# The modulation of an AdaLN layer moved from GpSimd to TensorE's column tiles

## The reference

```python
def adaln(cvec, w, b):
    m = jax.nn.silu(cvec) @ w + b          # w: 1024 x 3072
    return jnp.split(m, 3, axis=-1)

# layer i of the second block
sh_l, sc_l, gt_l = adaln(c, ada_w[i], ada_b[i])
h_lat = rms_norm(x_lat, norm_g[i]) * (1.0 + sc_l[:, None]) + sh_l[:, None]
# layer 0 also, for the context tokens:
sh_c, sc_c, gt_c = adaln(c_ctx, ada_w[i], ada_b[i])
```

## Time and profile before

| | |
|---|---|
| median of 3 runs | 2357.45 us (2355.15 to 2359.11) |
| the profiled execution | 2356.58 us, its span 2354.9 us |
| mean granted TensorE clock | 0.963 |
| PE busy | 2177.0 us, 92% of the span |
| DVE busy | 1459.5 us, 62% |
| ACT busy | 782.6 us, 33% |
| POOL busy | 285.3 us, 12%, 196 instructions |
| moved by DMA | 164.5 MB |

### The profile page before, as it was taken

The page is one execution under the profiler, slowest core; times in us unless marked ns, Lnnn a source line. Parts: engine busy times, 40 slices in busy tenths (PEclk is TensorE's granted clock), DMA queues, the critical chain, the costliest instruction groups (busy, mean ns, idle before and its releaser), DMA issues.

```text
span 2354.9 us, 26875 instructions
## 1 busy us (share of the span) xinstructions
PE 2177.0 (92%) x10667; PEld 1741.9 (74%) x10667; DVE 1459.5 (62%) x2256; ACT 782.6 (33%) x1161; POOL 285.3 (12%) x196
## 2 busy tenths in 40 slices
PE   6998878888999999799999999999999798999998
PEld 4876666566888886687888888887877577687876
DVE  5623778637848583477777777777777632443342
ACT  4362222334324333423333332233222233332232
POOL 0012666414224030000000000000000000000000
PEclk9998899998999999899999999999999799999998
DMA  4331111323434343111111111111111022023320
GB/s 139 99 89 37 45 38 53 90 88 109 126 110 132 115 129 87 45 54 45 46 46 48 51 45 47 52 45 46 45 47 53 18 89 81 28 85 85 87 82 37
DMA packets 311132, 164.54 MB, mean 70 GB/s; under 512 B 6268, under 2 KB 307938, under 8 KB 311010
## 3 DMA queue, kind: packets, MB, share of 16 engines
q1 hardware_dynamic: 311010, 162.85, 23.8%
HBM read 160.73 MB, written 2.10 MB: 69 GB/s over the span
## 4 chain that ended last, share of the span: by engine, by line
PE 72%; DVE 19%; issue 5%; ACT 3%; POOL 0%; SPq 0%; DMA 0%; DVEq 0%; ACTq 0%; POOLq 0%
PE bank L474 16%; PE bank L476 16%; PE bank L475 16%; DVE KC L1710 3%; DVE MT L1732 3%; DVE QC L1712 3%; DVE QQ L1717 2%; PE bank L819 2%; PE bank L509 2%; PE bank L493 1%; PE bank L491 1%; PE bank L492 1%; PE bank L885 1%; PE bank L798 1%; DVE PP L1725 1%
## 5 line engine op out<-in xcount | busy, mean ns | idle before, releaser
L1344 DVE TENSOR_TENSOR wl<-stage,wh 128x1024 fp32r<-128x1024 f32 (+1 forms) x248 | 311.7, 1258 | 661.9 <-ACT wh L947 661.8
L474 PE MATMUL bank<-hh,wh 128*128 128x512 f32 x1408 | 586.3, 416 | 30.6 <-DVE hl L1365 14.7
L947 ACT ACTIVATE wh<-stage 128x1024 fp32r<-128x1024 f32 (+1 forms) x248 | 260.1, 1050 | 964.3 <-PE bank L476 610.0
L476 PE MATMUL bank<-hh,wl 128*128 128x512 f32 x1408 | 554.4, 394 | 0.0
L475 PE MATMUL bank<-hl,wh 128*128 128x512 f32 x1408 | 553.1, 393 | 0.0
L474 PEld LDWEIGHTS bank<-hh,wh 128*128 128x128 f32 x1408 | 267.2, 190 | 97.2 <-issue 36.8
L476 PEld LDWEIGHTS bank<-hh,wl 128*128 128x128 f32 x1408 | 266.9, 190 | 58.9
L475 PEld LDWEIGHTS bank<-hl,wh 128*128 128x128 f32 x1408 | 268.3, 191 | 52.9 <-issue 4.3
L474 PE MATMUL bank<-gh,wh 128*128 128x512 f32 x432 | 179.4, 415 | 16.0 <-DVE gl L1573 6.6
L428 POOL TENSOR_TENSOR mprod<-stage,gs 128x1024 f32<-128x1024 f32 x64 | 130.8, 2044 | 465.6 <-DMA stage<-in_ada_w 460.7
L476 PE MATMUL bank<-gh,wl 128*128 128x512 f32 x432 | 170.6, 395 | 0.0
(11 more groups left out here) (305 smaller groups left out, 3188.3 us busy)
## 6 DMA issues: line engine op xcount, KB each, us to landing
stage<-in_hg_w_in SPq DMA_DIRECT2D x80, 512.0 KB, 3.6
stage<-in_ada_w SPq DMA_DIRECT2D x48, 512.0 KB, 3.6
stage<-in_w_up SPq DMA_DIRECT2D x44, 512.0 KB, 3.8
stage<-in_ft_w_in SPq DMA_DIRECT2D x32, 512.0 KB, 3.9
stage<-in_w_in SPq DMA_DIRECT2D x28, 512.0 KB, 3.8
stage<-in_w_down SPq DMA_DIRECT2D x16, 512.0 KB, 3.7
stage<-in_hg_w_out SPq DMA_DIRECT2D x16, 512.0 KB, 3.6
stage<-in_ft_w_out SPq DMA_DIRECT2D x16, 512.0 KB, 3.5
```

The lines of the kernel that those rows point to most:

```text
L474: pe.matmul(bank[t % NLIN][:], wh[:, s, k, :], xh[:, k, :], start=a, stop=False)
L476: mm = pe.matmul(bank[t % NLIN][:], wl[:, s, k, :], xh[:, k, :], start=False, stop=b)
L947: do(A.activation(wh[:, l % NSPLIT, 0:nk, :], stage[:, u["slot"], 0:nk, :], ACT.Copy), "hi_ready")
L1344: do(X.tensor_tensor(wl[:, l % NSPLIT, 0:nk, :], stage[:, u["slot"], 0:nk, :], wh[:, l % NSPLIT, 0:nk, :].bitcast(F32), ALU.subtract), f"s ...
```

## The change

GpSimd's program goes. A raw unit becomes a tile of 512 rows and 256 columns of `ada_w` (same bytes, pieces of 1 KB instead of 512 bytes); two of them, the upper and lower half of the rows, make a block, and there are 12 blocks a layer. `silp` holds the silu of both vectors as columns 0 and 1 of 32, the other 30 zero, for each of the eight row tiles. PE takes `silp` as the stationary operand with 32 columns and the raw weights as the moving operand with 256 columns, both plain f32; the four row tiles of a half go to four column tiles of the array (32 output partitions each), the second half accumulates on the first. ScalarE copies the 128 x 256 sums out of `bank[7]` (`mod_rows`), and two matmuls with the constant `pick` (`mod_columns`) add the four partial sums and turn rows into columns. PE frees the slot now. In the mixer a block stands in 12 of 32 steps and its column matmuls one step later; in the FFN a block stands between the two tiles of each of the first twelve pairs, and its column matmuls behind the next pair's first tile. ScalarE's copy stands behind the evacuation of the pair's second tile.

```diff
+BLOCKS = 12
-    raws = [dict(w="ada_w", layer=l, rows=(0, 8), col=j * P, lin=False, raw=l * 24 + j)
-            for l in range(2) for j in range(24)]
+    raws = [dict(w="ada_w", layer=l, rows=(4 * kh, 4), col=j * 2 * P, lin=False, raw=(l * BLOCKS + j) * 2 + kh)
+            for l in range(2) for j in range(BLOCKS) for kh in range(2)]
...
             for half in range(2):
                 add("w_up", (0, 8), half * FF + j * P, "h")
-            units.extend(late[:2 if j < 2 else 1])
-            late = late[2 if j < 2 else 1:]
+                if half == 0:
+                    units.extend(late[:2])
+                    late = late[2:]
...
+        MOD_STEP = {2 + (8 * j) // 3: j for j in range(BLOCKS)}
...
-        @block.gpsimd
-        def _(pool):
-            do = Own(pool, "pool_chain")
...
# PE, a raw unit
+                    j, kh = u["raw"] // 2, u["raw"] % 2
...
+                    pe.wait_ge(S(f"stage_in{slot}"), 16 * (u["load"] + 1))
+                    if kh == 0 and j:
+                        pe.wait_ge(S("mod_ev"), j)
+                    w = raw_view(u)
+                    for k in range(4):
+                        mm = pe.matmul(bank[7][32 * k:32 * k + 32, 0:2 * P], silp[:, 4 * kh + k, :], w[:, k, :],
+                                       start=(kh == 0), stop=(kh == 1))
+                    mm.then_inc(S(f"stage_free{slot}"), 1)
...
+            def mod_columns(j):
+                pe.wait_ge(S("mod_ev"), j + 1)
+                for i in range(2):
+                    c = 2 * P + 2 * (2 * j + i)
+                    mm = pe.matmul(bank[7][:, c:c + 2], modrow[:, j % 2, i * P:(i + 1) * P], pick, start=True, stop=True)
+                mm.then_inc(S("mod_mm"), 1)
...
             def modulation(step):
-                while not units[pos[0]]["lin"] and modulation_sums(units[pos[0]]["raw"] + 1) <= 1.3 * (step + 1):
-                    unit(units[pos[0]])
-                    pos[0] += 1
+                if step - 1 in MOD_STEP:
+                    mod_columns(MOD_STEP[step - 1])
+                if step in MOD_STEP:
+                    for _ in range(2):
+                        unit(units[pos[0]])
+                        pos[0] += 1
...
# PE, the FFN
-                    units_to(t0 + 2 * j + 1, ("h_ready", KT) if r == 0 and j == 0 else None)
+                    units_to(t0 + 2 * j, ("h_ready", KT) if r == 0 and j == 0 else None)
+                    if 1 <= pairs + j <= BLOCKS:
+                        mod_columns(BLOCKS + pairs + j - 1)
+                    units_to(t0 + 2 * j + 1)
...
# ScalarE
+            def mod_rows(j):
+                u = raw_last[j]
+                act.wait_ge(S(f"stage_free{u['slot']}"), u["load"] + 1)
+                if j >= 2:
+                    act.wait_ge(S("mod_mm"), j - 1)
+                do(A.activation(modrow[:, j % 2, :], bank[7][:, 0:2 * P], ACT.Copy), "mod_ev")
...
+                    if p < BLOCKS:
+                        mod_rows(BLOCKS + p)
```

More of the change, by code:

```diff
@@ L96, in host_constants @@
                                 np.sin(2 * np.pi * (np.outer(t, u[1:-1]) % T) / T)], 1)).astype(np.float32)
-    onecol = np.zeros((P, 31), np.float32)
-    onecol[:, 15] = 1.0
-    return {"cf": cf, "hm": hm, "dch": dch, "dtok": dtok, "onecol": onecol}
+    pick = np.zeros((P, 2), np.float32)
+    pick[np.arange(4) * 32, 0] = pick[np.arange(4) * 32 + 1, 1] = 1.0
+    return {"cf": cf, "hm": hm, "dch": dch, "dtok": dtok, "pick": pick}
 def make_units():
@@ L203, in build @@
         raw = at("raw", A0 + 56, [P, 2, T + 8])
-        mprod = at("mprod", A0 + 56, [P, KT, P])
-        mod = at("mod", A0 + 60.25, [P, 2, 2, P])
+        modrow = at("modrow", A0 + 60.25, [P, 2, 2 * P])
+        silp = at("silp", A0 + 73, [P, KT, 32])
         cst = at("cst", A0 + 62.25, [P, 2 * P])
@@ L273, in build @@
         bank = [ctx.enter_context(nc.psum_tensor(f"bank{i}", [P, 512], F32)) for i in range(8)]
+        mcol = bank[7][:, 2 * P:2 * P + 96]
         def vcol(name, i=0):
@@ L279, in build @@
         halfeps = small[:, 0:1]
-        onecol = small[:, 1:32]
+        pick = small[:, 1:3]
         ada = small[:, 32:128]
@@ L288, in build, with raw_view @@
         mx, nmx, den, rden = gs[:, 160:192], gs[:, 192:224], gs[:, 224:256], gs[:, 256:288]
-        silc = gs[:, 288:304]
         block = ctx.enter_context(nc.Block())
+        def raw_view(u):
+            return view(stage[:, u["slot"], 0, 0:1], [[2 * P, 4], [1, 2 * P]])
         def tile_last(t):
@@ L301, in build @@
         T_OUT, T_UP, T_HG, T_HO, T_FT = FIRST["w_out"], FIRST["w_up"], FIRST["hg_w_in"], FIRST["hg_w_out"], FIRST["ft_w_in"]
+        MOD_STEP = {2 + (8 * j) // 3: j for j in range(BLOCKS)}
+        raw_last = {u["raw"] // 2: u for u in units if not u["lin"]}
         ffn_tiles = []
@@ L355, in load @@
             def load(u):
-                w = d["ada_w_2"][u["layer"]] if u["w"] == "ada_w" else weights[u["w"]]
                 k0, nk = u["rows"]
+                if u["w"] == "ada_w":
+                    sp.dma_start(raw_view(u), d["ada_w_2"][u["layer"]][k0 * P:(k0 + nk) * P, u["col"]:u["col"] + 2 * P].rearrange(
+                        "(k p) c -> p k c", p=P)).then_inc(S(f"stage_in{u['slot']}"), 16)
+                    return
+                w = weights[u["w"]]
                 sp.dma_start(stage[:, u["slot"], 0:nk, :],
@@ L449, in unit @@
                 if not u["lin"]:
+                    j, kh = u["raw"] // 2, u["raw"] % 2
+                    if u["raw"] == 0:
+                        pe.wait_ge(S("silc_ready"), 2)
                     if u["raw"] == 24:
                         pe.wait_ge(S("ada0"), 1)
[L453 to L459, removed]
+                    pe.wait_ge(S(f"stage_in{slot}"), 16 * (u["load"] + 1))
[6 more added lines that the diff above has]
+                    mm.then_inc(S(f"stage_free{slot}"), 1)
                     return
@@ L710, in _ @@
             attention_tail(32)
+            modulation(32)
             weigh(7)
@@ L1105, in heads4, with modulated @@
                 return b[:].rearrange("p (h c) -> p h c", c=P)
+            def modulated(n):
+                if n in MOD_STEP:
+                    mod_rows(MOD_STEP[n])
             for c in range(TT):
@@ L1116, in _ @@
                 do(A.activation(G["xx"][:], heads4(bank[4]), ACT.Copy), "x1e")
+                modulated(8 * c)
                 for l in range(1, 7):
@@ L1121, in _ @@
                     weights(8 * c + l)
+                    modulated(8 * c + l)
                 act.wait_ge(S("uw"), c + 1)
@@ L1128, in _ @@
                 do(A.activation(oT[:, :, tok], heads4(bank[4]), ACT.Copy), "o_ev")
+                modulated(8 * c + 7)
             attention_tail(32)
@@ L1386, in _ @@
             do(X.memset(halfeps, EPS), "const_set")
+            do(X.memset(silp[:], 0.0), "silp_zero")
             for k in range(KT):
@@ L1576, in _ @@
             bias = ROWS["ada_b"][0]
-            dve.wait_ge(S("mod_mm"), modulation_sums(24))
-            do(X.tensor_tensor(ada[:, 0:48:2], bank[7][:, 0:48:2], V[:, bias:bias + 24], ALU.add))
-            do(X.tensor_tensor(ada[:, 1:32:2], bank[7][:, 1:32:2], V[:, bias:bias + 16], ALU.add), "ada0")
+            dve.wait_ge(S("mod_mm"), BLOCKS)
+            do(X.tensor_tensor(ada[:, 0:48:2], mcol[:, 0:48:2], V[:, bias:bias + 24], ALU.add))
+            do(X.tensor_tensor(ada[:, 1:32:2], mcol[:, 1:32:2], V[:, bias:bias + 16], ALU.add), "ada0")
             do.settle()
```

11 lines of the change are left out of this document (6 added, 5 removed).

## The result

The changed kernel takes 2336.09 us (median; 2334.99 to 2337.88), the kernel before on the same chip 2358.28 (2355.15 to 2361.14). The ratio is 0.9907, with a 95% interval of 0.989 to 0.9924: 0.9% faster, where 1.4% slower was forecast. 2336 is outside the range and about 1 us from what rival C gave.

A forecast was written before the change was run, and what follows sets the result against it. TensorE was taken to bound the FFN, and hand-offs between engines the mixer. FFN +35.7, mixer -4.5 and the round's end +1 summed to +32.2 us, giving 2390 us, 1.4% slower than 2357.45; range 2342 to 2404.

The forecast's parts named there:

- rival C: Raw blocks on TensorE: all four column tiles run together, 0.86 us a block, total 2335 us; chance 0.17.
- New PE work: Raw blocks in mixer and FFN: 3.43 us each, column tiles one after another; column matmuls 0.46 us (FFN) or 0.60 (mixer).
- GpSimd's work goes: Mixer: VectorE loses some 39 us of stretching, TensorE's idle time falls by 18 us; FFN gains nothing except at round ends.
- Old PE work goes: Old modulation-sum matmuls leave TensorE: 23.9 us less in the mixer, 11.0 us less in the FFN.
- The FFN's sum: FFN: 12 x (3.43 + 0.46) - 11.0 = +35.7 us, undamped because TensorE is full there.
- The mixer's sum: Mixer: 227.5 us TensorE work plus 29 idle, less 11 for a better clock, gives 245.5 against 250, -4.5 us.
- The loads and ScalarE: Weight loads and ScalarE's copies: loads covered by 5 us, column matmuls hardly covered, counted zero; first FFN round's end +1 us.

The follow-up runs named there:

- e1: Changed kernel with all eight row tiles of a block summed in column tile 0 instead of spread over four: 2392.72 us, 1.0143 of the kernel before.
- e2: Kernel before with GpSimd's three instructions a sum cut to one column of each tile, waits kept, modulation sums not computed: 2331.26 us, ratio 0.9886.
- e7: Changed kernel plus 40 rounds of GpSimd's old three operations on an unread buffer, in the mixer alone: 2352.67 us, 0.9973 of the kernel before.
- e5: Changed kernel with all 24 blocks of both layers in the mixer and none in the FFN: 2330.83 us, 0.9885 of the kernel before.
- e3: Changed kernel plus GpSimd's old three operations on an unread buffer, 40 rounds in the mixer, 24 in the FFN: 2373.06 us, 1.0061 of the kernel before.

## Why the prediction was wrong

**The step that failed** is *New PE work*: "I take 3.43, from the rows it is nearest to". The block measured 1.00 us. L606 did show that a narrow stationary is not faster by itself, and e1 confirms it: 3.57 us in one tile. It shows nothing of neighbours in different tiles, as the same paragraph says, and that was the question. The nearest row answered another one; column tiles ran side by side. With the block's price open by a factor of four, and every us of it worth 24 in the sum, the choice of the end decided the sign; the chance of 0.50 for one end and 0.17 for the other was more than rows bore out.

The Trainium skill (TensorE: Matmul & The Clock Gate, "Part 3: Packing small matmuls — row/col tiling") says that column tiles run concurrently. The runs agree: 1.93 times for two tiles and 3.57 for four, by the block widths above. The Trainium skill's one read port for the moving operand (SBUF — State Buffer, "Who interferes with whom") spoke for the forecast; four tiles with four different moving operands ran together all the same, so the measurement decides against that reading of the page.

**GpSimd's work goes**: right in its mechanism and nearly in its size. The three groups fell to the calm durations, 8.2 us less for L1551. From TensorE's waits 18 us were taken; e2 measured 21.3 in the mixer, of which 19.9 is idle time. That the stretching gives nothing in the FFN was right: 356.3 us before and in e2. The Trainium skill's exclusive lock (SBUF — State Buffer, "Who interferes with whom") fits e2 and e7, where the same VectorE group means 0.68 us with GpSimd nearly still and 1.26 with it at work.

**Old PE work goes**: right in the mixer. The parts add up: 330.8 - 21.3 (e2) - 23.9 + 17.7 (e5's step for 12 blocks) = 303.3 us of mixer, measured 299.8 and 304.4 in two executions of the same code. In the FFN's first part 356.3 - 11.0 = 345.3, and e5, which has no blocks there, stands at 348.0; 1.5 of these 2.7 us are longer waits at the rounds' ends (5.8 us against 4.3).

**The FFN's sum**, 12 x (block + columns) - 11.0, was right in form. Read from the timeline alone, the two cost 1.8 us on the mean: the gap of 1.7 and the 0.1 by which L459 then comes late. That gives 12 x 1.8 - 11.0 = +10.6, and 2.6 more at the rounds' ends make +13.2, where the first part measured +14.7; some 1.5 us stay open. The price of `mod_columns` by itself was right: where nothing waits, block and columns open 1.43 us, and the block has 1.00 of it, which leaves 0.43 where 0.46 was taken. What the sum left out are its waits and those at the rounds' ends.

**The mixer's sum** left 11 us to a better clock. The granted clock did rise, from 0.89 to 0.93 up to the last L598 and from 0.89 to 0.91 with w_out; with one tile it was 0.92, and the mixer measured 329.8, -1.0, against the forecast's -4.5. TensorE's busy time in the mixer, 190.8 us, is 6 under 203.0 - 23.9 + 12 x 1.48 = 196.9, as a better clock would make it. But the sum of lengths above closes within 4 us without such a term, so its size stays open between 0 and some 6 us, and the 11 is not shown.

**The loads and ScalarE**: "hardly covered, zero in the sum" was right. The waits of `mod_columns` came to 1.7 us in all, though the landing of `w_up` rose from 3.8 to 4.9 us over the whole span. The first round's end waits 2.97 us instead of 1.36, +1.6 where +1 was put down; all three rounds together wait 6.9 us instead of 4.3, and the forecast counted only the first.

## What to carry to other kernels

Small f32 matmuls whose outputs go to different column tiles of 32 ran side by side here when they were issued in turn: price them by the tile that has the most, not by their sum. Where a price is open between ends that decide the sign, and no row shows the situation itself, a row of something alike is no reason to choose an end; give the ends chances of their own, or expect little of the point. GpSimd's work off the critical path can still set the time through VectorE: TensorE's waits for the stretched VectorE lines, added up, came here within some 3 us of the 21 gained. And before a difference of a few us is given to an edit, compare the stretches that it does not touch, and their granted clock.

## What the runs showed of the hardware

- A block of eight matmuls, 32 columns stationary and 256 moving, f32: 3.57 us in one column tile, 1.85 in two, 1.00 in four. Each record still reads 379 ns (its median); only the spacing changes, four starting together where one started, so a group's width shows the overlap and its mean does not.
- Two GpSimd rounds in each of twelve pairs of the FFN cost 28 us in the profiled executions (e3 against e7), though VectorE is busy for only 280 of 457.5 us there: TensorE waits up to 1.6 us for a row copy and 7.8 us at the round's end.
- Two profiled executions of one mixer code differed by 4.6 us over some 300 (1.5%), where the four runs of the changed kernel differ by 2.9 us over 2336 (0.1%). TensorE's idle time was the same within 0.6 us; the clock was 0.90 and 0.91.
